# An attention loop on one Trainium2 core: mask and maximum fused, norm gains multiplied in on GpSimd, weights split in 512-column pieces, scores of two softmaxes alternated

## The reference, cut to what matters

```python
p = rmsnorm(x, g) @ w_in                      # q and z of layer 1
kv = rmsnorm(x, kv_norm_g) @ w_kv             # shared keys and values, keys and q with rotary
# per head (8) and block of 128 queries (8), two key/query pairs c of 64 columns each:
s[c] = q[c] @ k[c].T * 64 ** -0.5             # causal mask: -inf above the diagonal
w = softmax(s[0]) - lam * softmax(s[1])
o = head_rmsnorm(w @ v, subln) * (1 - lam_init)
x = x + (o * silu(z)) @ w_out
```

## Time and profile before

| | |
|---|---|
| runs | 2081.1, 2084.1, 2087.9 us (median 2084.1) |
| span of the profiled execution | 2078.4 us |
| median less that span (what lies around it) | 5.7 us |
| TensorE busy in the span | 1826.7 us, 88% |
| VectorE, ScalarE, GpSimd busy | 1153.2, 806.3, 379.9 us |
| mean granted TensorE clock | 0.928 |

### The profile page before, as it was taken

The page is one execution under the profiler, slowest core; times in us unless marked ns, Lnnn a source line. Parts: engine busy times, 40 slices in busy tenths (PEclk is TensorE's granted clock), DMA queues, the critical chain, the costliest instruction groups (busy, mean ns, idle before and its releaser), DMA issues. The chain is left out here.

```text
span 2078.4 us, 40295 instructions
## 1 busy us (share of the span) xinstructions
PE 1826.7 (88%) x13011; PEld 1669.8 (80%) x13011; DVE 1153.2 (55%) x3279; ACT 806.3 (39%) x2208; POOL 379.9 (18%) x823
## 2 busy tenths in 40 slices
PE   5499999999999675998999999999999688888598
PEld 4399999999999564998889898898989666665398
DVE  4443544443443354246767667676677566666533
ACT  5333333333333223033534435344353356666401
POOL 1021221221221121011312213122131100101101
PEclk8699999999999776999999999999999888989699
DMA  4213113113211134222011120111200267777522
GB/s 118 64 32 65 31 33 65 34 30 65 34 30 15 39 88 131 78 103 87 26 50 32 31 63 12 51 32 31 63 12 11 82 228 257 257 243 241 157 73 84
DMA packets 157012, 165.21 MB, mean 79 GB/s; under 512 B 12314, under 2 KB 134266, under 8 KB 156914
## 3 DMA queue, kind: packets, MB, share of 16 engines
q1 hardware_dynamic: 152610, 159.85, 26.2%
q0 software_dynamic: 1184, 4.23, 0.8%
q10 hardware_dynamic: 3120, 0.01, 0.1%
HBM read 138.69 MB, written 25.37 MB: 79 GB/s over the span
## 5 line engine op out<-in xcount | busy, mean ns | idle before, releaser
L809 PE MATMUL PS<-WH,XH 128*128 128x384 f32 (+3 forms) x1152 | 369.4, 321 | 1.8 <-DVE WORK L731 1.8
L809 PE MATMUL PS<-WL,XH 128*128 128x384 f32 (+3 forms) x1152 | 356.9, 310 | 0.0
L809 PE MATMUL PS<-WH,XL 128*128 128x384 f32 (+3 forms) x1152 | 356.6, 310 | 0.0
L809 PEld LDWEIGHTS PS<-WH,XH 128*128 128x128 f32 (+1 forms) x1152 | 208.1, 181 | 6.6 <-DVE WORK L731 2.2
L809 PEld LDWEIGHTS PS<-WL,XH 128*128 128x128 f32 (+1 forms) x1152 | 208.2, 181 | 4.1
L809 PEld LDWEIGHTS PS<-WH,XL 128*128 128x128 f32 (+1 forms) x1152 | 207.8, 180 | 4.6
L1432 PE MATMUL PS<-WH,XH 128*128 128x256 f32 (+1 forms) x576 | 166.2, 289 | 34.4 <-DVE WL L1305 28.6
L1831 PE MATMUL PS<-WH,XH 128*128 128x256 f32 (+1 forms) x576 | 173.6, 301 | 2.3 <-ACT WORK L1586 2.1
L1831 PE MATMUL PD<-WH,XH 128*128 128x256 f32 (+1 forms) x576 | 169.4, 294 | 2.9 <-PEq L142 2.9
L1831 PE MATMUL PS<-WL,XH 128*128 128x256 f32 (+1 forms) x576 | 167.4, 291 | 0.0
L1831 PE MATMUL PS<-WH,XL 128*128 128x256 f32 (+1 forms) x576 | 167.0, 290 | 0.0
(11 more groups left out here) (335 smaller groups left out, 4411.3 us busy)
## 6 DMA issues: line engine op xcount, KB each, us to landing
RAW<-in_cache_k SPq DMA_DIRECT2D x64, 512.0 KB, 4.5
WORK<-in_cache_v SPq DMA_DIRECT2D x64, 512.0 KB, 4.4
RAW<-in_w_in_a SPq DMA_DIRECT2D x40, 512.0 KB, 6.3
RAW<-in_w_in_b SPq DMA_DIRECT2D x16, 512.0 KB, 6.3
RAW<-in_w_kv SPq DMA_DIRECT2D x16, 512.0 KB, 5.2
out<-WORK SPq DMA_DIRECT2D x16, 512.0 KB, 2.9
WORK<-in_x_prompt SPq DMA_DIRECT2D x8, 512.0 KB, 4.9
WORK<-d_G SPq DMA_DIRECT2D x8, 512.0 KB
```

The source lines that it names most:

```text
L809: last = nc.tensor.matmul(bank[0:rows, 0:n], x[:, k, tt], reg(w)[:, k, :], start=(i == 0), stop=(i == 3 * KT - 1))
```

## The change

1. `cut` no longer multiplies with the gains. GpSimd does that in place in `RAW` (`gains`: per region two operations of 128x1024, the gain broadcast along 128 columns). It does region 0 of the next head at the top of `sweep2`, region 1 at the top of block t = 4, and region 1 of head 0 ahead of everything. ScalarE waits for `gn` where it waited for the load.
2. The split then goes over 4 contiguous pieces of 512 columns per region in place of 16 of 128, in blocks t = 0 to 3.
3. The scores' scale moves into `QTH`/`QTL` with a minus sign; mask, minimum and the write back become one `tensor_tensor_reduce` per softmax and block, over all columns, with a mask row `MT` (zeros, then the diagonal block).
4. `scores` alternates c within each pass and waits for both exponentials of the block before.
5. The first softmax's sum is no longer divided out ahead of the output norm: its square times EPS takes EPS's place in `root`. VectorE loses a reciprocal per block, ScalarE waits for `rr` ahead of the exponentials.

```diff
+            piece = lambda w, r, n: w[:, (r * CUTS + n) * KT * N // CUTS:(r * CUTS + n + 1) * KT * N // CUTS]
 scalar:
-                    def cut(r, k):
-                        for j, (_, _, g) in enumerate(PARTS[r]):
-                            cols = slice(j * P, (j + 1) * P)
-                            act.activation(reg(WH, r)[:, k, cols], reg(RAW, r)[:, k, cols], ACT.Copy,
-                                           scale=g[:, k:k + 1]).then_inc(hi[r], 1)
+                    def cut(r, n):
+                        act.activation(piece(WH, r, n), piece(RAW, r, n), ACT.Copy).then_inc(hi[r], 1)
...
                     def sweep2(h, last):
                         if not last:
-                            act.wait_ge(c_w[0], 32 * (h + 1))
+                            act.wait_ge(gn[0], 2 * (h + 1))
...
+                                act.wait_ge(rr, NT * h + max(t - 1, 0))
                                 for c in range(2):
                                     act.wait_ge(mxs, 2 * (NT * h + t) + c + 1)
                                     act.wait_ge(ww, NT * h + t)
                                     act.activation(PR[:, c, 0:(t + 1) * P], S[c][:, 0:(t + 1) * P], ACT.Exp,
-                                                   scale=ATTN_SCALE, bias=nm[:, c:c + 1],
-                                                   accum_out=sm[:, c:c + 1]).then_inc(ex, 1)
-                                if not last:
+                                                   scale=-1.0, bias=mx[:, c:c + 1],
+                                                   accum_out=sm[:, t % 2, c:c + 1]).then_inc(ex, 1)
+                                if not last and t < CUTS:
                                     cut(0, t)
 gpsimd:
                     def root(h, c):
                         b = c % 2
+                        pool.wait_ge(ex, 2 * (NT * h + c) + 2)
+                        apart(pool)
+                        links.link(g.tensor_scalar(e0[:, b:b + 1], sm[:, b, 0:1], sm[:, b, 0:1], EPS, ALU.mult, ALU.mult))
                         pool.wait_ge(sq, NT * h + c + 1)
...
+                    def gains(r, h):
+                        for j, (_, _, gain) in enumerate(PARTS[r]):
+                            raw = reg(RAW, r)[:, :, j * P:(j + 1) * P]
+                            g.tensor_tensor(raw, raw, gain[:, :].unsqueeze(2).to_broadcast([P, KT, P]), ALU.mult)\
+                             .then_inc(gn[r], 1)
...
                     def sweep2(h, last):
+                        if not last:
+                            pool.wait_ge(c_w[0], 32 * (h + 1))
+                            apart(pool)
+                            gains(0, h + 1)
                         for t in range(NB):
+                            if t == 4 and not last:
+                                pool.wait_ge(c_w[1], 32 * (h + 2))
+                                apart(pool)
+                                gains(1, h + 1)
...
+                    pool.wait_ge(c_w[1], 32)
+                    gains(1, 0)
+                    pool.wait_ge(lamD, 1)
 vector:
-                    def cut(r, k, h):
-                        for j, (_, _, g) in enumerate(PARTS[r]):
...
-                            v.scalar_tensor_tensor(reg(WL, r)[:, k, cols], reg(RAW, r)[:, k, cols], g[:, k:k + 1],
-                                                   reg(WH, r)[:, k, cols].bitcast(F32), ALU.mult, ALU.subtract)\
+                    def cut(r, n, h):
+                        dve.wait_ge(hi[r], CUTS * h + n + 1)
+                        v.tensor_tensor(piece(WL, r, n), piece(RAW, r, n), piece(WH, r, n).bitcast(F32),
+                                        ALU.subtract).then_inc(lo[r], 1)
...
-                                    links.link(v.tensor_tensor(S[c][:, n - P:n], S[c][:, n - P:n],
-                                                               cst[:, C_MB:C_MB + P], ALU.add))
-                                    links.link(v.tensor_reduce(mx[:, c:c + 1], S[c][:, 0:n], AX, ALU.max, negate=True))
-                                    v.tensor_scalar(nm[:, c:c + 1], mx[:, c:c + 1], ATTN_SCALE, None, ALU.mult)\
-                                     .then_inc(mxs, 1)
+                                    apart(dve)
+                                    v.tensor_tensor_reduce(S[c][:, 0:n], S[c][:, 0:n], MT[:, SEQ - n:SEQ], 1.0, BIG,
+                                                           ALU.add, ALU.min, mx[:, c:c + 1]).then_inc(mxs, 1)
...
-                                v.reciprocal(rc[:, b:b + 1], sm[:, 0:1])
 tensor:
-                        for c in range(2):
-                            pe.wait_ge(ex, 2 * NT * h + max(2 * t - 1 + c, 0))
-                            rows = slice(DK * c, DK * c + DK)
-                            for at in range(0, width, 512):
-                                kk = slice(at, min(at + 512, width))
...
+                        pe.wait_ge(ex, 2 * NT * h + 2 * t)
+                        for at in range(0, width, 512):
+                            kk = slice(at, min(at + 512, width))
+                            for i, (q, k) in enumerate(((QTH, KTH), (QTH, KTL), (QTL, KTH))):
+                                for c in range(2):
+                                    rows = slice(DK * c, DK * c + DK)
```

More of the change, by code:

```diff
@@ L64, in constants @@
     c[:, C_MA:C_MA + P] = np.where(r[:, None] <= r[None, :], 0.0, BIG)
-    c[:, C_MB:C_MB + P] = np.where(r[None, :] <= r[:, None], 0.0, -BIG)
+    c[:, C_MB:C_MB + P] = np.where(r[None, :] <= r[:, None], 0.0, BIG)
     inv = (np.float32(10000.0) ** (-(np.arange(HALF, dtype=np.float32) / np.float32(HALF)))).astype(np.float32)
@@ L1479, in attention_phase @@
             take = area(AREA - 2 * SEQ)
+            N1 = 2 * P
+            spare = YX[:, KT * TOK:NB * D]
             QKR = take(2, 2, P)
-            RA, RB = take(8, HALF), take(8, HALF)
+            RA, RB = (spare[:, k * N1:(k + 1) * N1].rearrange("p (g c) -> p g c", c=HALF) for k in range(2))
             V = take(NT, P)
@@ L1485, in attention_phase @@
             EZ, ZC, GZ = take(2, P), take(2, P), take(2, P)
-            Y, JK = take(2, P), take(2, P)
+            Y, JK = take(2, P), spare[:, 2 * N1:3 * N1].rearrange("p (b c) -> p b c", b=2)
             SM = take(4, P)
             SL = take(P)
-            LQ = take(4, DK)
+            MT = take(SEQ)
+            LQ = PR[:, 0, 0:4 * DK].rearrange("p (j d) -> p j d", j=4)
             le, nl = take(2), LAM[:, :]
-            mx, nm, sm, rc, ssq, var, rs, rr2 = (take(2) for _ in range(8))
+            mx, ssq, e0, var, rr2 = (take(2) for _ in range(5))
+            sm = take(2, 2)
             cf = take(1)
@@ L1592, in squares @@
                         act.wait_ge(av, NT * h + c + 1)
-                        act.activation(JK[:, c % 2, :], B_O[:, 0:P], ACT.Square, scale=rc[:, c % 2:c % 2 + 1],
+                        act.activation(JK[:, c % 2, :], B_O[:, 0:P], ACT.Square,
                                        accum_out=ssq[:, c % 2:c % 2 + 1]).then_inc(sq, 1)
@@ L1615, in sweep1 @@
                                 act.wait_ge(tr[c % 2], 4 * h + c // 2 + 1)
-                                act.activation(QTH[:, c * P:(c + 1) * P], BK[2 + c % 2][:, 0:P], ACT.Copy)
+                                act.activation(QTH[:, c * P:(c + 1) * P], BK[2 + c % 2][:, 0:P], ACT.Copy,
+                                               scale=-ATTN_SCALE)
                                 act.activation(KTH[:, c * P:(c + 1) * P], BK[2 + c % 2][:, P:2 * P], ACT.Copy)\
@@ L1820, in tail @@
                         o_transposed(h, NT - 1)
-                    heads(dve, sweep1, sweep2, tail, links, 9 + 8 * 2 * 2 + 16)
+                    heads(dve, sweep1, sweep2, tail, links, 9 + 16)
                 @block.tensor
@@ L1837, in scores @@
                         width = (t // 2 + 1) * 2 * P
-                        for c in range(2):
-                            pe.wait_ge(ex, 2 * NT * h + max(2 * t - 1 + c, 0))
-                            rows = slice(DK * c, DK * c + DK)
-                            for at in range(0, width, 512):
-                                kk = slice(at, min(at + 512, width))
-                                i = 0
-                                for q, k in ((QTH, KTH), (QTH, KTL), (QTL, KTH)):
+                        pe.wait_ge(ex, 2 * NT * h + 2 * t)
[4 more added lines that the diff above has]
+                                    rows = slice(DK * c, DK * c + DK)
                                     x = nc.tensor.matmul(S[c][:, kk], q[rows, t * P:(t + 1) * P], k[rows, kk],
                                                          start=(i == 0), stop=(i == 2))
-                                    i += 1
-                            x.then_inc(sc, 1)
+                                    if i == 2 and kk.stop == width:
+                                        x.then_inc(sc, 1)
                     def turn_weights(h, c):
```

43 lines of the change are left out of this document (22 added, 21 removed).

## The result

The changed kernel takes 2024.25 us (median of four runs, 2019.65 to 2027.78), the kernel before 2082.73 in the same session: 0.9708 of it, 95% interval 0.969 to 0.9726.

What follows compares the result with a forecast made beforehand. TensorE, busy 88% of 2078.4 us, was taken as the bound, with VectorE stopping at the loop's jump. Terms -35.5 - 18.2 - 7.8 + 10.2 + 10.5 + 2.5 = -38.3 gave 2046 us, range 2028 to 2072.

Steps and rivals of the forecast that it cites:

- fewer instructions, stop gone: VectorE's attention loop turn falls from 201 to 137 instructions, stays resident, no stop at the jump in heads 1-6: -35.5 us.
- order: Alternated score matmuls save the second softmax's late entry, 0.57 us, in blocks 4 to 7 of eight heads: -18.2 us.
- shorter way to the weights: One fused operation replaces three per softmax, and no cuts ahead of the blend in blocks 4 to 7: -7.8 us.
- all that was put at nothing: ScalarE's wider copies, the scale in `QTH`, `root`'s small operations and mask setup lie under projections: no cost.
- gains, both places: GpSimd's gain operations delay region 0 at the top of `sweep2`, +10.2 us, and region 1 in block 4, +10.5 us.
- head 0's start: GpSimd's first gains, ahead of the key copies, block VectorE's lambda and rotation operations: +2.5 us, bounds 0 and 4.9.
- the price of the gains: One GpSimd gain operation of 128x1024 was taken at 2.4 us, with bounds 2.1 and 3.7.
- the gains are hidden after all: Rival: the gains at both places cost nothing, giving 2025 us; chance 0.08.
- TensorE is what is waited for in these blocks, so I take all: In blocks 4 to 7 the alternated scores were credited with their full upper bound, -18.2 us.
- the stop stays: Rival: VectorE's loop is still too long, giving -5 in place of -35.5 and 2068 us; chance 0.10.
- No overlap today: Rival: the two softmaxes' score matmuls run one after the other now, so alternating saves 52 us, 2012 us; chance 0.01.
- The clock does not fall in the loop: Answers a rival: the `gn` wait at each `scores(0)` lowers TensorE's clock, +12 to +24, 2058 to 2070 us; chance 0.15.

Runs made afterwards that it cites:

- run 5: The kernel before with 36 one-column memsets more on VectorE ahead of the loop, nothing in the loop changed: 2051.6 us.
- run 2: The changed kernel with GpSimd's four gain operations per loop turn touching one column, so gains are left out of heads 1 to 7: 2020.3 us.
- run 7: The changed kernel with a third gain operation at each place, over half of the second one's columns: 2037.0 us.
- run 12: The kernel before with 36 memsets ahead of the loop and the scores alternated, nothing else: 2049.8 us.
- run 8: The changed kernel with GpSimd's second region 0 gain operation after the rotation and head 0's first cut made with the gains as before: 2057.1 us.
- run 4: The changed kernel with 68 one-column memsets more per turn of VectorE's loop: 2026.4 us.
- 11: The kernel of run 8 with 36 memsets ahead of the loop: 2017.2 us.
- run 1: The changed kernel with only the order of the score matmuls and their wait put back: 2039.7 us.

## Why the prediction was wrong, step by step

"Heads" and "start" against the terms of the sum:

| step | predicted | measured | from |
|---|---|---|---|
| fewer instructions, stop gone | -35.5 | -35.1 | run 5 less before |
| order, and shorter way to the weights (with all that was put at nothing) | -18.2 - 7.8 | -32.4 | run 2 less run 5 |
| gains, both places | +10.2 + 10.5 | +4.9 | changed less run 2 |
| head 0's start | +2.5 | +4.5 | start |
| sum | -38.3 | -58.1 | |

**The step that failed first is the price of the gains**, "I take 2.4, the same width" in the two steps on region 0 and region 1: 1.90 was measured, below even the lower bound of 2.1 made from the earlier trace rows, and both places together cost 4.9 us where the sum had 20.7. For region 1 the mechanism was right: with the pair at about the price assumed, block 5 of run 7 is 1.39 us longer than without gains (run 2), where the prediction had 1.5. At 1.90 the gains of region 1 end almost as the chain needs them, and cost 0.14 us per head. For region 0 the place was wrong too. The prediction let the rotation slow GpSimd and the wait appear at `project_values(1)`; VectorE was held instead, and the wait stands ahead of `scores(0)`. It costs 0.56 us per head, and 1.0 at run 7's price, where the prediction had 1.45. The rival "the gains are hidden after all", 2025 us at a chance of 0.08, had the nearest number, by luck: they are not hidden but cost a quarter of what the sum gave them, and the order with the shorter way gave 6.4 us more than the sum had.

**The second is that order and chain were added up.** "TensorE is what is waited for in these blocks, so I take all" fell with run 12: on the kernel before, the order gives next to nothing, because TensorE then waits for VectorE's way from scores to weights. Only with the fused operation, which shortens that way, is it worth 15.3. And the -7.8 for that way was read from head 7, which lacks the cuts but has the old chain: it could show what the cuts cost and not what a shorter chain gives. The cuts turned out at 2.2, the fused operation at 17.4, both measured within the change; such numbers must not be added to the 15.3, since each is the loss of one with the others there.

**The stop**: its going, its size (-35.5 against -35.1) and the clock behind it were right, the reason only in part. It is VectorE's code at the jump, but not the count of a turn: a turn that touches three pieces of 8 KB runs on, one that touches four stops. That the changed kernel has this gain is luck: by the count some 6 records are to spare, and with 12 more ahead of the loop it was gone (run 8). So the chance of 0.10 for "the stop stays" rested on a limit "between 126 and 201" that run 4, at 221, does not show; a dozen more instructions ahead of the loop would have made it come true.

**The rest.** Head 0's start, +4.5, is within its bounds of 0 and 4.9: one of the waits ahead of `scores(0)` lies in it, and without it and without GpSimd's first gains the start is back at 37.1 and 36.7 (runs 8 and 11). No overlap today (0.01) fell with run 1: 15.3 and not 52. Nor did the matmuls start in the order of issue: in block 6 of head 2 of the kernel before, the second softmax's first one starts at 0.57 us, ahead of the first softmax's fourth (0.80), though it is issued behind all six. The clock does not fall in the loop. The twelve score matmuls of block 6 start within 1.27 us, as "what would show it" had it with 1.3:

```profile
1180.72 0.50 PE L1869 MATMUL PD<-WH,QTR 64*128 64x512 f32 x2
...
1181.99 0.40 PE L1869 MATMUL PD<-WH,QTR 64*128 64x512 f32 x2
```

Three of its other signs failed with the price of the gains: `scores(0)` to `scores(2)` takes 7.6 to 7.7 us and not 9.6, block 5 is 0.14 us longer than in head 7 and not 1 to 2, and there is no pause ahead of `project_values(1)`.

## What to carry to other kernels

Where an engine stops for nothing at a loop's jump, find from the loads in the trace how many pieces of code its turn touches and where in a piece it begins; moving the loop by a few instructions is the cheapest thing to try, and every edit ahead of it may bring the stop back. Two edits that shorten neighbours on one chain are priced together: one alone may show nothing. And where a cost hangs on whether work ends before it is wanted, a fifth off the price of an operation can take most of it away (1.39 us per head at run 7's price in block 5, 0.14 at the real one), so keep both ends of it in the range.

## What the runs showed that was not expected

The same 36 instructions ahead of a loop took 34 us off the kernel before and 40 off run 8 (35 and 38 by "heads"). A GpSimd multiplication of 128x1024 with a broadcast second input takes 1.90 us, against 2.40 in the earlier trace rows with two full inputs and another output type; which of the two makes the difference was not tried. VectorE's two-input SBUF operations were held until GpSimd's ended, for 1.7 us (L1757) and 0.7 (L1835), and GpSimd's gate operation (L1702) until VectorE's blend ended, while the fused operation with one input in PSUM kept its 0.83 us under the gains.
